# Moving the ring of low weights by 32 bytes in a decoder layer that multiplies in split float32

## The kernel before, in words

| stage | blocks | form |
|---|---|---|
| w_in, tiles 0 to 7 (`a_raw`) | 128 | pair |
| w_in, tiles 8 to 79 (`a_raw`, `a_in`) | 1152 | triple |
| GLU (`glu_in`) | 32 | pair |
| branches (`o_hg`, `o_sb`, `o_s5`) | 192 | triple |
| out (`a_in`) | 256 | pair |
| up (`h2`) | 1408 | pair |
| down (`act`) | 660 | pair |
| down, last tile (`act`) | 44 | triple |

## Time and profile before

### The profile page before, as it was taken

One profiled execution on the slowest core, in us unless ns is written; L12 is line 12 of the kernel. 1 busy time (PEld: TensorE's weight loads), 2 busy tenths in 40 slices (PEclk: granted clock), 3 DMA queues, 4 the chain that ended last, 5 costly groups with the idle time before them and its releaser, 6 DMA issues.

```text
span 1389.6 us, 27921 instructions
## 1 busy us (share of the span) xinstructions
PE 1384.8 (100%) x9886; PEld 1278.0 (92%) x9886; DVE 1034.8 (74%) x1427; ACT 755.1 (54%) x1056; POOL 142.9 (10%) x187
## 2 busy tenths in 40 slices
PE   9999999999999999999999999999999999999999
PEld 8999999999999999988888888888888888888888
DVE  7999857789888778776687777777777776445453
ACT  7575666753543554555655555555555554344432
POOL 1200000000000014322111111111111110000000
DMA  8655545455555556766566656565656656666663
GB/s 284 191 186 178 181 156 176 140 171 184 181 189 174 183 177 215 232 189 189 177 202 195 185 194 191 186 185 196 192 188 191 194 174 198 211 188 201 196 205 110
DMA packets 76513, 261.70 MB, mean 188 GB/s; under 512 B 8800, under 2 KB 10368, under 8 KB 76448
## 3 DMA queue, kind: packets, MB, share of 16 engines
q1 hardware_dynamic: 74304, 255.89, 58.1%
q0 software_dynamic: 1424, 4.37, 1.0%
q10 hardware_dynamic: 720, 0.53, 0.1%
HBM read 258.66 MB, written 2.10 MB: 188 GB/s over the span
## 4 chain that ended last, share of the span: by engine, by line
PE 98%; DMA 1%; SPq 0%; ACT 0%; DVE 0%; issue 0%
PE bank L377 40%; PE bank L391 29%; PE bank L379 21%; PE bank L417 5%; PE pair L436 1%; PE bank L402 1%; DMA x_first<-xT 0%; DMA raw<-w_in 0%; PE pair L573 0%; PE pair L442 0%; SPq L299 0%; PE pair L544 0%; SPq L319 0%; DVE w_lo L1077 0%; ACT w_hi L744 0%; ACT a_raw L910 0%
## 5 line engine op out<-in xcount | busy, mean ns | idle before, releaser
L1077 DVE TENSOR_TENSOR w_lo<-raw,w_hi 128x1024 fp32r<-128x1024 f32 x496 | 585.3, 1190 | 289.9 <-ACT w_hi L744 286.9
L744 ACT ACTIVATE w_hi<-raw 128x1024 fp32r<-128x1024 f32 x496 | 508.8, 1031 | 409.1 <-PE bank L379 192.2
L377 PE MATMUL bank<-h,w_hi 128*128 128x512 f32 x1408 | 485.3, 388 | 0.0
L379 PE MATMUL bank<-h,w_lo 128*128 128x256 f32 x1408 | 394.2, 280 | 0.0
L391 PE MATMUL bank<-a_in,w_hi 128*128 128x256 f32 x2048 | 364.3, 281 | 0.0
L391 PEld LDWEIGHTS bank<-a_in,w_hi 128*128 128x128 f32 x2048 | 312.8, 188 | 3.1 <-issue 2.1
L377 PEld LDWEIGHTS bank<-h,w_hi 128*128 128x128 f32 x1408 | 264.0, 187 | 55.1
L391 PE MATMUL bank<-a_in,w_lo 128*128 128x256 f32 x1024 | 286.5, 280 | 0.0
L379 PEld LDWEIGHTS bank<-h,w_lo 128*128 128x128 f32 x1408 | 264.1, 188 | 0.0
L377 PE MATMUL bank<-act,w_hi 128*128 128x512 f32 x660 | 227.4, 388 | 0.0
L391 PEld LDWEIGHTS bank<-a_in,w_lo 128*128 128x128 f32 x1024 | 192.8, 188 | 0.0
(11 more groups left out here) (234 smaller groups left out, 1395.8 us busy)
## 6 DMA issues: line engine op xcount, KB each, us to landing
raw<-w_up SPq DMA_DIRECT2D x176, 512.0 KB, 3.7
raw<-w_in SPq DMA_DIRECT2D x156, 512.0 KB, 4.2
raw<-w_down SPq DMA_DIRECT2D x80, 512.0 KB, 4.3
raw<-w_out SPq DMA_DIRECT2D x32, 512.0 KB, 4.1
raw<-w_br SPq DMA_DIRECT2D x16, 512.0 KB, 3.6
raw<-w_br SPq DMA_DIRECT2D x16, 256.0 KB, 3.6
raw<-w_down SPq DMA_DIRECT2D x16, 256.0 KB, 2.7
x_first<-xT SPq DMA_DIRECT2D x8, 256.0 KB, 6.2
```

What stands on the lines that cost most here:

```text
L377: pe.matmul(bank[b][:, :], w[:, k * P:(k + 1) * P], a.rearrange("p a t -> p (a t)"), start=first and n == 0, stop=False, skip_group_check= ...
L379: mm = pe.matmul(bank[b][:, 0:SEQ], l[:, k * P:(k + 1) * P], a[:, 0, :], start=False, stop=last and n == len(blocks) - 1, skip_group_check ...
L744: act_e.activation(w_hi[s][:, 0:blocks * P], raw[s][:, 0:blocks * P], ACT.Copy).then_inc(hi_ready, 1)
L1077: ve.tensor_tensor(w_lo[s][:, w], raw[s][:, w], w_hi[s][:, w].bitcast(F32), ALU.subtract).then_inc(lo_ready, 1)
```

## The change

`apart_weights` grows from 8 to 16 float32 in each partition (32 to 64 bytes), and `apart`, behind the small tensors, shrinks from 32 to 24 (128 to 96 bytes). No instruction is added, removed or reordered; every instruction has the same shape, and only start addresses differ.

```
-        sb("apart_weights", [P, 8])
+        sb("apart_weights", [P, 16])
         w_lo = [sb(f"w_lo{s}", [P, PIECE * P], F32R) for s in range(RING)]
...
-        sb("apart", [P, 32])
+        sb("apart", [P, 24])
```

## The result

The changed kernel takes 1403.49 us (median of 5, 1402.96 to 1403.76) against 1391.62 us: 1.0085 times as long, 95% interval 1.0074 to 1.0097. The forecast was 1391.6 with 1377 to 1402; the rival "relation 224 is the worse one for 512 elements" stood at 1404.3. The profiled execution's span grew from 1389.6 to 1401.9 us, by 12.3.

A forecast was written before the change was run, and what follows sets the result against it. PE was taken as the bound, time being matmuls times their step. Every term of the change was taken at 0, so the forecast stayed at 1391.2 us on the profiled execution, 1391.6 as a median, range 1377 to 1402.

The forecast's parts named there:

- relation 224 is the worse one for 512 elements: Pair form's w_hi matmul above a w_lo load gets 5.1 ns dearer: 12.7 us, 1404.3 us; chance 0.14.
- What bounds the kernel, and through what a change of addresses acts: PE, idle 0.05 us in 1367.87: time is matmuls times step, and addresses can act only through the step.
- a sign against all of it: A PE that waits for w_lo would overturn the whole forecast.
- The loads of w_lo, "I take no change": 3872 low-weight loads beside PE's matmuls: moving them changes no step, since relations 0 and 32 look alike; 0.
- The few instructions beside `lower`: Mixers' matmuls, sole example of relation 224: 512 elements look 5.1 ns dearer, 256 cheaper by up to 7; five instructions.
- The pace: Each form has two paces 2.2 ns a block apart, kept from stage start; up and down slow costs 4.5 us.
- The small tensors, "I take 0": PE reads only ones, two_rows, eye and lower of them, in the mixers' products; moving them costs 0.
- Each of the 754 small matmuls got slower by 10 ns: Bound for moving the small tensors: 7.5 us if all small matmuls slowed so; nothing pointed to it.
- the dearer matmul: Rival of a dearer 512-element matmul in pair form, 1399 to 1405 us; chance 0.14.

The follow-up runs named there:

- e4: PE alone, layer left out: pair-form blocks at all 64 combinations of high and low weights' places modulo 256; 340.0 to 353.5 ns a block.
- e8: PE alone, layer left out: triple-form blocks at all 64 combinations of high and low weights' places; 340.0 to 373.3 ns a block.
- e7: PE alone: three layouts, pair-form blocks before and after a norm2-like product with ones and root at 32 place combinations; at (224, 0) 344.5, 346.7 or 353.3 ns a block.
- e11: Kernel before with the norm2 product left out, PE's wait kept, output not the layer's; 1395.86 us, ratio 1.0031.
- e5: Kernel before with rings and activations placed as in the changed kernel, small tensors keeping their old places modulo 256; 1403.14 us, ratio 1.0083.
- e2: Kernel before with only the small tensors between low ring and activations 32 bytes further; 1410.13 us, ratio 1.0135.
- e10: Kernel before with low ring and activations 32 bytes further, small tensors padded (ones 224 past activations), most triple-form low weights another 64 bytes further; 1379.79 us.
- e1: Kernel before with the low ring 32 bytes further and everything declared behind it following; 1401.94 us, ratio 1.0075.
- e6: e1 with the norm2 product left out, PE's wait kept, output not the layer's; 1381.91 us, ratio 0.9928.

## Why the prediction was wrong

- *What bounds the kernel, and through what a change of addresses acts*: right. The time is the number of matmuls times their step, PE's waits behind the first 20 us are one of 0.2 us, DVE's w_lo stayed at 1224 to 1225 ns. The head's waits for w_lo did grow, by 1.3 us, which the prediction had as a sign against all of it; they explain 0.7 of the 12.3 us at the most.
- *The loads of w_lo, "I take no change"*: this step failed: taken at 0, it is 4.4 ns a block in up and down, 9.2 us, and about 1.1 us in the other stages of pair form. It was taken from the earlier trace rows, where relations 0 and 32 look alike. That comparison asks whether one matmul has another length than its neighbour, but the streams can settle into a pattern over several blocks, and both relations together with what ran before set its length. It shows in e4's and e8's maps, and in the steps of 227, 231 and 235 ns in turn. The few instructions beside `lower`, which I set aside, gave 5.1 ns more for the 512-element matmul; the changed kernel has 4.4 more in up and down, in that matmul.
- *The rival "relation 224 is the worse one"*: right in place and side, and 1404.3 against 1403.5. Its price was too high by a little for up and down and by more for out (2.2 ns), and its reason is not a property of 224 alone: at high 128, low 32 and low 0 run alike, at high 96 low 32 is the faster one, by 3.4 ns (e4). That the sum came within 0.8 us is luck in part: it has nothing for the triple form (1.3 us) and the head (0.7), and too much for the pair form (12.7 against 10.3).
- *The pace*: that a form runs at more than one pace at the same addresses was right. That it has two was not (32 triple blocks of the kernel before run at 356.7 ns), nor that a stage keeps the one it starts with: in the kernel before, up starts at 346.7 and turns to 344.4 at the norm2 product. The sizing was wrong as well: I allowed only the two paces seen, so the most it could cost was 4.5 us. Another relation has other paces, here 348.9 (and 353.3 behind some seeds of e7), both above the two. Of the 4.4 ns in up and down, 2.2 is the difference between what (224, 0) and (224, 32) take in the out stages and in e4, and 2.2 is what the norm2 product had given the kernel before, by e11, and none of e7's 32 seeds gives at (224, 32).
- *The small tensors, "I take 0"*: right for this change (e5 against the changed kernel: 1403.14 and 1403.49), and wrong as a rule. In e2 their 32 bytes cost 18.5 us through one product of two instructions. "Each of the 754 small matmuls got slower by 10 ns" counted only their own time, not what they leave behind. The list of what PE reads of them also left out `root`, the moving operand of just that product.
- *The range* ended at 1402, because the dearer matmul was given only 0.14.

What stays open is what in PE or SBUF makes the pattern. The paces of the full kernels, 340.0, 344.4, 346.7, 348.9, 350.0, 351.1, 353.3 and 356.7, stand whole multiples of 1.11 ns above 340.0 within rounding (e4 also has some that do not, 349.3 and 351.8). In their traces the pair form's paces of 340.0, 346.7, 350.0 and 353.3 repeat block after block, and those of 344.4 and 348.9 every three blocks. That looks like waits counted in clock ticks; it is argued, not shown. Whether the 1377.6 to 1382.3 of e10 are stretches that fall differently from run to run was not looked at either.

## What to carry to other kernels

When PE is busy all the time and still runs above its streaming time, measure its pace as window length over matmuls, stage by stage: two stages with the same instructions and two paces say that a better one may be had by moving tensors, here 0.7% for three lines of padding. Map the relations of stationary and moving operands with PE alone first; one kernel holds 64 of them, and in pair form its numbers carried over to the full kernels' out stages within 0.1 ns. A cell is only one of the paces that its placement can have, as the triple form showed in e10: 340.0 in the map, 340.0 or 356.7 in the kernel. Then look at what PE does just before each long stage, since a single small product can hold the next 700 us at the slower pace, and judge no shift of addresses by the total alone: e1 and the changed kernel agree to about 0.1%, with 340.0 against 348.9 ns a block in out and 350.0 against 348.9 in up.

## What was not expected of the hardware

- Matmuls whose stationary operand is reloaded each time ran at 340.0 to 353.5 ns for 768 fp32r elements in pair form and 340.0 to 373.3 in triple form, by nothing but the places of the operands modulo 256 bytes and what PE ran before, at a granted clock of 1.00 in every window shown (e4, e8).
- The same stream at the same addresses can have three stable paces (344.5, 346.7 and 353.3 ns at (224, 0), e7). The kernel before, e11 and e2 each hold one of them through the 2068 blocks of up and down.
- A product of 0.24 us decides between them; leaving it out changed the time by -20.0 us in one layout (e6 against e1) and by +4.3 in another (e11).
